# Selection rounds by tile, and w_o scaled behind the last rotary step, in a two-layer decoder trunk on one core

## What is computed

```python
score = jnp.einsum('bqhs,bqh->bqs', rel, wb)              # indexer, causal
_, sel = lax.top_k(score, topk)                           # topk = 128
...
ya = swa_with_sinks(qa, ka, va, sinks)
yb = dsa_sparse_attention(qb, kb, vb, qi, ki, wi)
y = jnp.concatenate([rms_norm(ya, g_a), rms_norm(yb, g_b)], -1)
return y @ w_o
...
x = layer_norm(ALPHA * x + (1.0 + gt1) * y, ln1_g[l], ln1_b[l])
h = x * (1.0 + sc2) + sh2
y = swiglu(h, w_gate[l], w_up[l], w_down[l])
```

## Time and profile before

| | |
|---|---|
| median of 3 runs | 1410.78 us (1409.65 to 1414.73) |
| profiled execution | 1408.33 us, span 1406.6 us, mean granted TensorE clock 0.966 |
| TensorE busy | 1294.3 us, 92% of the span |
| VectorE, ScalarE, GpSimd busy | 836.6, 507.3 and 242.8 us |
| attention loop of layer 0, layer 1 | about 166 to 293 us, 841 to 964 us |

### The profile page before, as it was taken

How to read it: one execution, slowest core, us unless ns; L and a number is a source line. 1 busy time by engine, 2 the same in 40 slices (tenths; PEclk the granted TensorE clock), 3 DMA queues, 4 the chain that set the end, 5 groups by cost and what they waited for, 6 DMA issues and landing times.

```text
span 1406.6 us, 18546 instructions
## 1 busy us (share of the span) xinstructions
PE 1294.3 (92%) x6392; PEld 1068.6 (76%) x6392; DVE 836.6 (59%) x1472; ACT 507.3 (36%) x1041; POOL 242.8 (17%) x255
## 2 busy tenths in 40 slices
PE   2799898899999999999999999799999999999996
PEld 2686777677888878888778678677798877888775
DVE  6668787728877766433176798842853345333337
ACT  0435355724433311223134555572443321132310
POOL 1080027610111100000004403762000000000001
PEclk9897899999999999999999989989999999999998
DMA  8563200412777835232124120011242323233211
GB/s 322 215 199 118 79 1 16 152 44 83 261 239 270 261 127 193 90 98 95 60 75 134 32 88 18 1 46 45 69 127 91 103 89 105 85 110 95 98 45 60
DMA packets 44272, 156.17 MB, mean 111 GB/s; under 512 B 5808, under 2 KB 5808, under 8 KB 44208
## 3 DMA queue, kind: packets, MB, share of 16 engines
q1 hardware_dynamic: 30528, 109.07, 23.3%
q0 software_dynamic: 12672, 46.14, 9.8%
q10 hardware_dynamic: 1008, 0.12, 0.1%
HBM read 153.21 MB, written 2.10 MB: 110 GB/s over the span
## 4 chain that ended last, share of the span: by engine, by line
PE 67%; DVE 13%; POOL 7%; issue 4%; DMA 4%; ACT 4%; SPq 0%; DVEq 0%; ACTq 0%; POOLq 0%
PE bank L528 20%; PE bank L529 20%; PE bank L530 20%; DMA w_raw<-in_weights 3%; POOL w_raw L424 2%; DVE w_lo L1242 2%; PE bank L683 2%; PE bank L704 1%; DMA ada_w<-in_w_ada 1%; DVE top L1366 1%; DVE xs L1463 1%; PE bank L740 1%; POOL w_lo L432 1%; DVE ada_acc L1265 1%; DVE ztmp L1460 1%
## 5 line engine op out<-in xcount | busy, mean ns | idle before, releaser
L528 PE MATMUL bank<-hT_hi,w_hi 128*128 128x512 f32 (+1 forms) x768 | 287.2, 374 | 2.2 <-issue 1.5
L529 PE MATMUL bank<-hT_lo,w_hi 128*128 128x512 f32 (+1 forms) x768 | 285.9, 372 | 0.0
L530 PE MATMUL bank<-hT_hi,w_lo 128*128 128x512 f32 (+1 forms) x768 | 285.9, 372 | 0.0
L1614 DVE TENSOR_TENSOR w_lo<-w_raw,w_hi 128x1024 fp32r<-128x1024 f32 x88 | 107.8, 1225 | 146.4 <-ACT w_hi L1152 146.4
L528 PE MATMUL bank<-w_hi,hT_hi 128*128 128x512 f32 (+2 forms) x448 | 172.7, 386 | 14.5 <-DVE hT_lo L1327 6.8
L985 ACT ACTIVATE w_hi<-w_raw 128x1024 fp32r<-128x1024 f32 x96 | 100.4, 1058 | 230.2 <-PE bank L530 227.1
L528 PEld LDWEIGHTS bank<-hT_hi,w_hi 128*128 128x128 f32 x768 | 145.2, 189 | 28.3 <-issue 2.3
L529 PE MATMUL bank<-w_lo,hT_hi 128*128 128x512 f32 (+2 forms) x448 | 166.5, 372 | 0.0
L530 PE MATMUL bank<-w_hi,hT_lo 128*128 128x512 f32 (+2 forms) x448 | 166.1, 371 | 0.0
L530 PEld LDWEIGHTS bank<-hT_hi,w_lo 128*128 128x128 f32 x768 | 145.1, 189 | 25.4
L529 PEld LDWEIGHTS bank<-hT_lo,w_hi 128*128 128x128 f32 x768 | 145.1, 189 | 25.0
(11 more groups left out here) (147 smaller groups left out, 1921.6 us busy)
## 6 DMA issues: line engine op xcount, KB each, us to landing
w_raw<-in_weights SPq DMA_DIRECT2D x184, 512.0 KB, 3.4
ada_w<-in_w_ada POOLq DMA_DIRECT2D x80, 512.0 KB, 5.1
ada_w<-in_w_ada SPq DMA_DIRECT2D x16, 512.0 KB, 5.3
xs<-in_x SPq DMA_DIRECT2D x4, 512.0 KB, 9.8
g_row<-in_ln_row POOLq DMA_DIRECT2D x4, 512.0 KB, 4.6
b_row<-in_ln_row POOLq DMA_DIRECT2D x4, 512.0 KB, 5.3
trunk_out<-xs SPq DMA_DIRECT2D x8, 256.0 KB, 2.0
modb<-in_b_ada ACTq DMA_DIRECT2D x1, 48.0 KB, 3.7
```

What stands on the lines that cost most here:

```text
L528: pe.matmul(dst, a_hi, b_hi, start=first, stop=False)
L529: pe.matmul(dst, a_hi, b_lo, start=False, stop=False)
L530: return pe.matmul(dst, a_lo, b_hi, start=False, stop=last)
L1614: nc.vector.tensor_tensor(w_lo[:, s, :], w_raw[:, s, :], w_hi[:, s, :].bitcast(F32), ALU.subtract).then_inc(lo_ready, 1)
```

## The change

Three things are changed, all in the attention loop, in both layers.

The rounds are split by tile. `ROUND_TILES` gives the steps: 0, 3, ... 15 for all three tiles, 18, 21, ... 36 for tiles 3 and 1, and 41, 43, ... 53 for tile 2 alone. In a step with a round the maxima are taken ahead of the mask and the replacements behind it. `MASKS_AT` turns the scores of tiles 3 and 1 into masks at step 37 and those of tile 2 at step 54. Waits go by the last step of the same tile (`top_step`).

The eight scalings of `w_o` go from steps 32, 34, 36, 40, 46, 51, 56, 61 to 39, 44, 49, 54, 58, 60, 62, 64. The transposes of the last rotated tile go from step 41 to 45, with ScalarE's copy.

```diff
-QB_AT = tuple(r + 3 for r in ROPE_AT)
+QB_AT = tuple(r + 3 for r in ROPE_AT[:-1]) + (ROPE_AT[-1] + 7,)
...
-GAIN_AT = (32, 34, 36, 40, 46, 51, 56, 61)
+GAIN_AT = (39, 44, 49, 54, 58, 60, 62, 64)
...
-MASKS_AT = 40
 EARLY_ROUNDS = 3
+ROUND_TILES = {3 * n: (IDX_TILES if n < 6 else (3, 1)) for n in range(TOPK // 8 - EARLY_ROUNDS)}
+ROUND_TILES.update({41 + 2 * n: (2,) for n in range(TOPK // 8 - EARLY_ROUNDS - 6)})
+MASKS_AT = {37: (3, 1), 54: (2,)}
...
             def attention(l):
-                done = EARLY_ROUNDS
                 for i in range(64 + LAG_SPLIT):
+                    for t in ROUND_TILES.get(i, ()):
+                        top_max(t)
                     if i < 64:
                         u, h = i // 8, i % 8
                         mask_scores(l, u, h)
                         if h == 7 and UNITS[u][0] == "A":
                             sink_difference(l, u)
-                    if i < MASKS_AT:
-                        upto = EARLY_ROUNDS + (TOPK // 8 - EARLY_ROUNDS) * (i + 1) // MASKS_AT
-                        top_rounds(done, upto)
-                        done = upto
-                        if i == MASKS_AT - 1:
-                            top_masks()
+                    for t in ROUND_TILES.get(i, ()):
+                        top_replace(t)
+                    for t in MASKS_AT.get(i, ()):
+                        top_mask(t)
```

More of the change, by code:

```diff
@@ L1224, in _ @@
             steps = [0]
+            top_step = {t: 0 for t in IDX_TILES}
             conv = [0]
-            ada = [0]
             def step(ins):
@@ L1355, in add_index_head, with top_replace @@
                     step(nc.vector.tensor_tensor(own, own, band[:, P:2 * P], ALU.add))
+                    top_step[t] = steps[0]
+            def top_max(t):
+                sc = scores[:, SC_AT[t]:SC_AT[t] + (t + 1) * P]
+                dve.wait_ge(dve_step, top_step[t])
+                nc.vector.max(top8[:, t, :], sc).then_inc(dve_step, 1)
+                steps[0] += 1
+                top_step[t] = steps[0]
+            def top_replace(t):
+                sc = scores[:, SC_AT[t]:SC_AT[t] + (t + 1) * P]
+                dve.wait_ge(dve_step, top_step[t])
+                nc.vector.match_replace(out=sc, in_to_replace=top8[:, t, :], in_values=sc, imm_value=TAKEN)\
+                    .then_inc(dve_step, 1)
+                steps[0] += 1
+                top_step[t] = steps[0]
             def top_rounds(r0, r1):
@@ L1360, in top_rounds @@
                     for t in IDX_TILES:
-                        sc = scores[:, SC_AT[t]:SC_AT[t] + (t + 1) * P]
-                        steps[0] += 1
-                        if r > 0:
-                            dve.wait_ge(dve_step, steps[0] - 3)
-                        nc.vector.max(top8[:, t, :], sc).then_inc(dve_step, 1)
-                    for t in IDX_TILES:
-                        sc = scores[:, SC_AT[t]:SC_AT[t] + (t + 1) * P]
-                        steps[0] += 1
-                        dve.wait_ge(dve_step, steps[0] - 3)
-                        nc.vector.match_replace(out=sc, in_to_replace=top8[:, t, :], in_values=sc, imm_value=TAKEN)\
-                            .then_inc(dve_step, 1)
-            def top_masks():
-                dve.wait_ge(dve_step, steps[0])
-                step(nc.vector.tensor_scalar(scores[:], scores[:], CUT, NEG, ALU.is_gt, ALU.mult))
+                        top_max(t)
+                    for t in IDX_TILES:
+                        top_replace(t)
+            def top_mask(t):
+                sc = scores[:, SC_AT[t]:SC_AT[t] + (t + 1) * P]
+                dve.wait_ge(dve_step, top_step[t])
+                step(nc.vector.tensor_scalar(sc, sc, CUT, NEG, ALU.is_gt, ALU.mult))
             def mask_scores(l, u, h):
```

## The result

The changed kernel takes 1394.82 us (median of 4 runs, 1392.57 to 1399.46), beside 1410.22 us for the kernel before in the same set (4 runs, 1408.98 to 1414.73). The ratio is 0.990, 95% interval 0.9879 to 0.9920: 15.4 us faster, which is small, 1.1%, but clear of the noise. A later set gave 1393.91 us for the changed kernel beside 1406.87 us for the one before, ratio 0.9908 (0.9892 to 0.9923). The profiled execution took 1394.32 us with a span of 1392.6 us, at a mean granted clock of 0.970.

A forecast was written before the change was run, and what follows sets the result against it. TensorE bounds the kernel as a whole, with holes from masks, the rotary step and late roots. Savings of 6.5 us in layer 0 and 7.8 in layer 1, together 14.3, take 1410.8 to 1396.5 us; 8-in-10 range 1388.5 to 1403.5.

The forecast's parts named there:

- (a): Rounds at heads 0 to 37: less VectorE work ahead of masks saves 2.2 us a layer, between 0.9 and 3.7.
- (b): Last rotary step without scalings ahead of it: saves 4.2 us in layer 1, 0.4 in layer 0.
- (c): Last rotated tile's transposes from head 41 to 45: 0.4 us saved in layer 0, 0.4 lost in layer 1.
- the 1.2 GHz stretch: Slow TensorE clock around head 42, taken as unchanged; bounds 3 us lost or gained a layer.
- (d): Tile 2's rounds inside the B heads: overfull VectorE loses 2.6 us in layer 0, 0 in layer 1.
- The 8.4 us: Layer 0's B heads: seven VectorE sums each waiting half a GpSimd low half, instead of 2.5 us; total then 1402.4.
- (e): Late scalings, heads 58 to 64: transfer waits hidden, late TensorE waits gone; saves 6.1 us in layer 0, 1.8 in layer 1.
- GpSimd's list: GpSimd's work from layer 0's third root to its sixth: 34.3 us, plus 10 of waits, ending at 281.
- rival 2: Slower: late GpSimd scalings hold ScalarE's first four conversions in both layers, 23.2 us more, 1419.7 us; 6%.
- Rival 1: VectorE too full in layer 0's B heads, sums wait for GpSimd, little gain: 1405 us; 13%.
- rival 4: More comes back: no fall to 1.2 GHz around head 42, VectorE's overload fills waits: 1387.9 us; 14%.

The follow-up runs named there:

- no_round_at_0: Changed kernel with rounds of heads 0 to 36 three heads later in both layers, masks of tiles 3 and 1 at head 39: 1390.57 us, ratio 0.9886.
- l1_later: Changed kernel with rounds of heads 0 to 36 moved to heads 3 to 39 in layer 1 alone, masks at 39: 1392.31 us, ratio 0.9876.
- max_behind: Changed kernel with a round's maxima again behind the head's mask, right ahead of the replacements: 1397.04 us, ratio 0.9899.
- transposes_41: Changed kernel with the last rotated tile's transposes and copy-out back at head 41: 1394.21 us, ratio 0.9911.
- the repeat: Changed kernel run once more, unedited, as control of the later set: 1393.91 us, ratio 0.9908.
- all_tiles_early: Changed kernel with tile 2 kept in all 13 rounds at heads 0 to 36, its mask at 37, none in the B heads: 1398.13 us, ratio 0.9919.
- rounds_only: Kernel before with only the new rounds, split by tile and moved; scalings and transposes as before: 1403.27 us, ratio 0.9957.
- late_gains_old: Changed kernel with the last four scalings back at heads 46, 51, 56, 61 and the first four at 39, 41, 43, 45: 1405.92 us, ratio 0.9991.

## Why the prediction was right, and where its steps were not

The forecast was 1396.5 us for a measured 1394.82, and the sum of the loops 14.3 us for 13.9. But layer 0 gave 8.1 instead of 6.5 and layer 1 5.8 instead of 7.8; two errors of about 2 us cancelled, by luck. So did what the forecast left out, +1.6, −2.7 and +1.1 us outside the loops, where "everything behind the loop" was to "move along whole". The time came out better than the steps deserve.

**(a), layer 1, is the step that failed**: "Rounds that move forward from heads 3 to 39 to heads 0 to 36 start in VectorE's idle time at the head of the loop; I cost that at nothing." In layer 1 there is no idle time in front of the first masks: VectorE comes from a low half with no gap, TensorE waits for it, more of the stage runs at 1.2 GHz, and it costs 4.7 us. `no_round_at_0` and `l1_later` show it. In layer 0 the same stage loses 0.7 us at most. For all of (a) layer 1 was to give 2.2 us and gave −4.7 + 4.5 = −0.2.

**(a), heads 6 to 40, was mis-sized.** I took 2.2 of at most 3.7 us of mask waits; net of the first stage, layer 0 gave 3.6, nearly the whole bound, and layer 1 4.5 behind its loss. The split of the block, which I put beside the smaller work, adds nothing once tile 2 is gone (`max_behind`).

**(b) and (c)** were put at 0.8 us in layer 0 and 3.8 in layer 1, and gave 0.9 and 5.1. The rotary step starts as forecast, and from its start to its root takes 3.94 us in both layers (4.31 in layer 1 before), so the 0.4 us for the collision with VectorE's mask pass were right. ScalarE's first conversion waits 0.71 and 0.58 us for its scaling, for 0.7 forecast. The step "so I leave the 1.2 GHz stretch as it is" was wrong: in layer 1 the clock there is 1.00, and the two waits of 2.41 and 0.84 us did not bring it down; in layer 0 the mean granted clock of 0.69 over 11 us means some 6.8 us at 1.2 GHz, and the 0.79 over 8 us now (232 to 240, then 1.00) some 3.4. Nor did I see the price of the move to head 45, the waits at head 48; with these in, (c) is worth nothing beside the other two (`transposes_41`).

**(d)**: 1.4 us lost in layer 0's B heads (2.1 in the repeat) for a forecast of 2.6, and 1.2 in layer 1 for 0. Only a part is the rounds': `all_tiles_early`, without them, loses 0.9 in layer 0. The excess of 2.5 us that one sum had before has nearly gone. These are the first, the second and the seventh sum of the changed kernel's B heads:

```profile
240.08 1.37 DVE L1267 SCALAR_TENSOR_TENSOR ada_acc<-ada_w,cc,ada_acc 128x1024 f32<-128x1024 f32 x1
...
244.49 1.28 DVE L1267 SCALAR_TENSOR_TENSOR ada_acc<-ada_w,cc,ada_acc 128x1024 f32<-128x1024 f32 x1
...
264.00 1.72 DVE L1267 SCALAR_TENSOR_TENSOR ada_acc<-ada_w,cc,ada_acc 128x1024 f32<-128x1024 f32 x1
```

The sum at 240.08 met a low half (238.00 to 240.36), was held 0.1 us and ended 1.1 us behind it. The Trainium skill, "SBUF — State Buffer", section "SBUF: two separate sides", has such instructions lock each other out whole, and for a sum that begins inside a low half the rows agree. The sum at 264.00 is another case: it met a root (263.89 to 264.47) and then a scaling (from 264.46), and was held 0.45 us. Not by the root: beside the same root, without a scaling behind it, the sum took 1.28 us in `rounds_only` and in `late_gains_old`. The 8.4 us that I had worked out for seven sums did not come, since the other five took 1.27 or 1.28 us. In `late_gains_old` two sums are held for long:

```profile
239.60 3.92 DVE L1267 SCALAR_TENSOR_TENSOR ada_acc<-ada_w,cc,ada_acc 128x1024 f32<-128x1024 f32 x1
...
255.35 3.60 DVE L1267 SCALAR_TENSOR_TENSOR ada_acc<-ada_w,cc,ada_acc 128x1024 f32<-128x1024 f32 x1
```

Both met low halves (239.97 to 242.33 and 255.52 to 257.87) and took 2.65 and 2.33 us over the 1.27. By their rows these sums start first, by 0.37 and 0.17 us, as did the one of before (267.27 against 267.58), and yet it is the sum that waits.

**(e)** was put at 6.1 and 1.8 us and gave 5.1 and 2.0. GpSimd's list came out close: 9.4 us of waits instead of the 10 counted, and 46.0 us from the third root to the end of the sixth (232.97 to 278.94) for 44.4 forecast. But ScalarE asks for that root 2.0 us before it is there. "So TensorE's 2.15 and 2.83 us go" was too much; 1.74 stayed. (d) and (e) together were to give 3.5 and 1.8 us and gave 3.7 and 0.8. The reason that I gave, transfers under work, is not the whole of it. What `late_gains_old` shows is that order and distance on GpSimd matter as well: a root behind two scalings holds ScalarE and then TensorE (3.13 us in layer 1), and low halves that fall on sums hold VectorE (2.55 us at head 48 of layer 0). The first is rival 2, the ping-pong on GpSimd, priced there at 23.2 us; the changed kernel's spacing avoids both, and the two with the waits for transfers cost 1405.92 − 1393.91 = 12.0 us.

**Signs and rivals.** Of the signs named in advance the start of the rotary step, the end of the 6.22 us wait and of the waits for transfers, and a full VectorE in layer 0's B heads (25.23 of 27 us) came. Three failed: the waits for masks are under 2 us in layer 0 (0.4) but 3.7 in layer 1; ScalarE waits 1.27 us at its fourth conversion; 1.74 of the late waits stayed. Rival 1 did not happen. Of rival 4 one half came true: the clock around head 42 no longer falls in layer 1, and in layer 0 about half of the slow stretch stayed. The best kernel by its ratio is `l1_later`, 0.9876, below before for certain, and `no_round_at_0` (0.9886) can't be told from it; its interval and those of the changed kernel (0.9900 and 0.9908) touch, so 3 us over the changed kernel rest on the stage of 4.7 us that the traces show, more than on the medians.
